# A second pair of output chunks computed with seven products, its weight sums made by accumulating transfers

## The chip, the cores and the metric

One Trainium2 chip, one core. The metric is the device time of one execution in microseconds. The program is one layer written out by hand for the five engines: TensorE (PE), VectorE (DVE), ScalarE (ACT), GpSimd (POOL) and SyncE (SP), which issues nearly all transfers.

## The reference, cut to what matters

```python
proj = jnp.einsum('bsd,de->bse', rmsnorm(x, g_norm), w_in)        # 256 x 2048 by 2048 x 7704
# ... two kinds of attention give o_moba and o_nsa, each 256 x 1024
y_moba = rmsnorm(o_moba * jax.nn.silu(m_z), g_out_moba)
y_nsa = rmsnorm(o_nsa * jax.nn.silu(n_z), g_out_nsa)
y = jnp.concatenate([y_moba, y_nsa], axis=-1)                      # 256 x 2048
return x + jnp.einsum('bse,ed->bsd', y, w_out)                     # 2048 x 2048 weights; then a last norm
```

All in float32. S = 256 tokens (two tiles m of 128), model width 2048.

## The kernel before, in words

**Units.** Both large products are cut into column chunks of 512: fifteen of w_in (chunks 0 to 14; 11 to 14 are the z chunks) and four of w_out (chunks NC to NC + 3, NC = 15, so 15 to 18 in the code, output chunks 0 to 3 in words). A unit (c, g) is chunk c by 512 rows of weights: 1 MB, and 24 matmuls of 128x512, since each of its 2 m x 4 k products is done in three terms. A weight w is split into w_hi (ACT rounds it, L1081) and w_lo = w - w_hi (DVE, L1430); x and y are split likewise; `three_products` (L692) multiplies hi by hi, hi by lo and lo by hi. So each unit goes: SP loads it into one of three buffers of w_raw once the `lo` of three units before is done (L485), ACT does `hi(u)`, DVE does `lo(u)`, PE multiplies. The split buffers w_hi and w_lo hold three places, taken in the order of RING.

**Pairs.** Where two chunks a and b form a pair, the first 512 rows of weights of both ((a, 0) and (b, 0), eight products of 6 matmuls each) are done by a Strassen-Winograd scheme with seven (`seven`, L771; P1 to P7). It needs sums of the four weight blocks B11, B12, B21, B22 (512 KB each), which DVE forms (`t1` to `t4`, L1713 to L1726), and sums of the four blocks of x or y (`x_sums`, `y_sums`). Its seven weight operands are split by `block_hi` (ACT, L1138) and `block_lo` (DVE, L1708). Partial products that both chunks need are copied out of PSUM by `mid_out_` (ACT, L1149) and added later (`mid_add`, DVE). Before the change four pairs exist: nq, Z1, Z2 and OUT_PAIR (output chunks 2 and 3).

**Slots.** Every engine runs a loop over slots (L1030, L1310, L1830) and within a slot a fixed order of calls. An engine's queue is strictly in order, so the place of a call in the loop decides what it waits behind. In general ACT and DVE round a unit in the slot given by `rounded_at` (L139), two slots ahead of PE. The stretch of the change is slots 55 to 64:

- slots 55 to 59: the last z units (14, g) on PE; the first half of y is scaled, transposed by PE in rounds (0, hg, m) (`y_round_`), multiplied with g by DVE (`y_times_g`, L1741), rounded by ACT (`y_hi`, L1281), and its remainder taken by DVE (`y_residual`, L1754). At the end of slot 59 DVE reads chunk 14 (`scaled`, L1635), ACT applies Silu (L1168), POOL multiplies with the attention's output (L651).
- slots 60 to 67: output units (0,0), (0,1), (1,0), (1,1), then (0,2), (0,3), (1,2), (1,3). Units with g of 2 or 3 need the second half of y, whose squares (L1278), root on POOL (L656 to L658), `y_scale` (L1728) and four rounds (1, hg, m) come in slots 60 to 63, two rounds at the end of slot 62 and two at the end of 63. `unit` waits for `ylo_done` and `lo_ready` (L753, L758).
- from slot 65: OUT_PAIR and its other units. The residual x is loaded into acc (= Q) at L575, and each chunk's sum is added to it (`residual`, L1763).

Of the kernel before, what the change touches and what calls it, by code (L numbers as in the profile page):

```python
# [116 lines left out]
def unit_at(slot):  # L117
# [9 lines left out]
    if slot >= NPROJ:  # L127
        c, g = OUT_UNITS[slot - NPROJ]
        return UNIT_NO[NC + c, g]
# [5 lines left out]
              41: 40, 42: 41, 43: 42, 44: 43, 45: 44, 46: 45, 47: 46, 49: 47, 50: 48, 52: 49, 53: 50, 54: 51, 55: 52, 56: 53, 57: 54, 58: 55,  # L135
              66: 61, 67: 62, 68: 63, 69: 64, 70: 65, 71: 66, 72: 67}


def rounded_at(slot):  # L139
# [4 lines left out]
    return slot - 4 if 60 <= slot < 65 else ROUNDED_AT.get(slot)  # L144
# [117 lines left out]
def heads_done(j):  # L262
# [14 lines left out]
            62: [(1, 0, 0), (1, 0, 1)], 63: [(1, 1, 0), (1, 1, 1)]}  # L277
# [10 lines left out]
def build_layer(nc, x, positions, inv_freq, w_in, g_norm, pe_ck, pe_cv, w_ck1, w_ck2, w_cv1, w_cv2,  # L288
# [4 lines left out]
    with ExitStack() as ctx:  # L293
# [3 lines left out]
        def sem(name):  # L297
# [1670 lines left out]
```

## Time and profile before

| | us |
|---|---|
| median of 3 executions | 495.52 (495.48 to 495.67) |
| the profiled execution | 495.6 |
| its span, first to last instruction | 493.8 |
| PE busy in it | 485.6, 98% of the span |
| DVE, ACT, POOL busy | 354.7, 261.9, 64.1 |
| mean granted TensorE clock | 0.998 |

The span is the part that the rows below divide; the execution's own time is 1.8 us longer. Times in the timeline count from the span's start. A busy time of PE can be longer than the distance between two starts, because matmuls overlap in the array.

### The profile page before, as it was taken

What the parts mean: (1) busy time and instruction counts of PE and PEld (TensorE: products, weight loads), DVE (VectorE), ACT (ScalarE), POOL (GpSimd) and SP (SyncE); (2) the same over time, 40 slices, a digit from 0 to 9 for tenths busy, and PEclk for the clock granted to TensorE, in tenths of its full rate; (3) what the DMA queues carried; (4) which work ended last, traced back from release to release, by engine and by line L of the source; (5) the groups of instructions that cost most, each with busy time, mean ns of one, the idle gap of its engine ahead of it and who ended that gap; (6) DMA issues with size and microseconds to landing.
All of it is one profiled execution on the core that took longest, in us unless ns stands there. A gap on an engine that the chain in (4) does not pass through costs nothing.

```text
span 493.8 us, 6550 instructions
## 1 busy us (share of the span) xinstructions
PE 485.6 (98%) x2514; PEld 403.9 (82%) x2514; DVE 354.7 (72%) x564; ACT 261.9 (53%) x374; POOL 64.1 (13%) x66
## 2 busy tenths in 40 slices
PE   9999999999999999999999999999999999999994
PEld 8887787877788888888888888888888888888883
DVE  5888855932699958775587887765887767888644
ACT  5886453642656535645544455664665664366422
POOL 2340100100112202000020200000322240040120
PEclk9999999999999999999999999999999999999999
DMA  8979894577476442433544724448247679543404
GB/s 291 335 264 383 319 330 146 197 251 260 134 270 193 171 171 85 171 129 128 171 141 158 256 61 157 140 151 304 85 144 299 240 260 360 166 150 107 147 1 170
DMA packets 56783, 97.50 MB, mean 197 GB/s; under 512 B 4560, under 2 KB 15408, under 8 KB 56368
## 3 DMA queue, kind: packets, MB, share of 16 engines
q1 hardware_dynamic: 54544, 96.03, 55.9%
q10 hardware_dynamic: 2208, 1.06, 0.9%
q8 instruction: 20, 0.33, 0.3%
q14 instruction: 11, 0.09, 0.0%
HBM read 93.93 MB, written 2.10 MB: 194 GB/s over the span
## 4 chain that ended last, share of the span: by engine, by line
PE 97%; issue 1%; DVE 0%; ACT 0%; POOL 0%; POOLq 0%; ACTq 0%; DVEq 0%
PE proj L694 26%; PE proj L696 26%; PE proj L695 26%; PE b_o L1001 4%; PE b_t L675 2%; PE b_p L970 2%; PE proj L727 2%; PE b_s L871 2%; PE proj L733 1%; PE proj L738 1%; PE proj L1021 1%; PE b_s L696 1%; PE b_s L694 1%; PE b_s L695 1%; PE b_p L675 0%
## 5 line engine op out<-in xcount | busy, mean ns | idle before, releaser
L1430 DVE TENSOR_TENSOR w_lo<-w_raw,w_hi 128x2048 fp32r<-128x2048 f32 x65 | 149.6, 2304 | 64.4 <-ACT w_hi L1081 64.3
L694 PE MATMUL proj<-w_hi,xT_hi 128*128 128x512 f32 (+1 forms) x490 | 192.6, 393 | 0.0
L696 PE MATMUL proj<-w_hi,xT_lo 128*128 128x512 f32 (+1 forms) x490 | 190.7, 389 | 0.0
L695 PE MATMUL proj<-w_lo,xT_hi 128*128 128x512 f32 (+1 forms) x490 | 190.5, 389 | 0.0
L1081 ACT ACTIVATE w_hi<-w_raw 128x2048 fp32r<-128x2048 f32 x65 | 124.1, 1912 | 32.8 <-PE proj L696 20.4
L694 PEld LDWEIGHTS proj<-w_hi,xT_hi 128*128 128x128 f32 x490 | 92.1, 188 | 20.2 <-issue 2.0
L696 PEld LDWEIGHTS proj<-w_hi,xT_lo 128*128 128x128 f32 x490 | 92.0, 188 | 19.5
L695 PEld LDWEIGHTS proj<-w_lo,xT_hi 128*128 128x128 f32 x490 | 92.1, 188 | 18.0
L1232 ACT ACTIVATE pT<-b_p 128x512 f32<-128x512 f32 (+2 forms) x24 | 11.7, 489 | 51.7 <-PE b_p L970 51.7
L642 POOL TENSOR_TENSOR rope_a<-rope_a,rope_b 128x512 f32<-128x512 f32 (+1 forms) x12 | 15.0, 1274 | 165.0 <-DVE rope_b L1517 165.0
L1711 DVE TENSOR_TENSOR w_lo<-blk_b,w_hi 128x1024 fp32r<-128x1024 f32 x16 | 19.8, 1235 | 18.3 <-ACT w_hi L1147 18.3
L694 PE MATMUL proj<-w_hi,ymT_hi 128*128 128x512 f32 x78 | 30.6, 393 | 0.0
L696 PE MATMUL proj<-w_hi,ymT_lo 128*128 128x512 f32 x78 | 30.4, 389 | 0.0
L695 PE MATMUL proj<-w_lo,ymT_hi 128*128 128x512 f32 x78 | 30.4, 389 | 0.0
L1147 ACT ACTIVATE w_hi<-blk_b 128x1024 fp32r<-128x1024 f32 x16 | 16.9, 1054 | 17.2 <-DVE blk_b L1715 11.5
L1226 ACT ACTIVATE prob<-prob,nmx 128x256 f32<-128x256 f32 (+1 forms) x48 | 21.3, 448 | 6.7 <-DVE nmx L1613 6.7
L1609 DVE CUSTOM_DVE_ANT_0 prob<-b_s,mask 128x256 f32<-128x256 f32 (+1 forms) x48 | 15.1, 352 | 8.1 <-PE b_s L696 8.1
L664 POOL TENSOR_TENSOR Q<-Q,KV 128x512 f32<-128x512 f32 x6 | 10.5, 1767 | 56.6 <-ACT rope_c L1293 56.6
L696 PEld LDWEIGHTS proj<-w_hi,ymT_lo 128*128 128x128 f32 x78 | 14.6, 188 | 3.1
L694 PEld LDWEIGHTS proj<-w_hi,ymT_hi 128*128 128x128 f32 x78 | 14.7, 188 | 2.9
L695 PEld LDWEIGHTS proj<-w_lo,ymT_hi 128*128 128x128 f32 x78 | 14.6, 188 | 2.9
L651 POOL TENSOR_TENSOR xo<-xo,rope_a 128x512 f32<-128x512 f32 x4 | 7.7, 1934 | 69.8 <-DVE xo L1633 63.7
(271 smaller groups left out, 568.4 us busy)
## 6 DMA issues: line engine op xcount, KB each, us to landing
w_raw<-in_w_in_dram SPq DMA_DIRECT2D x51, 1024.0 KB, 4.9
w_raw<-in_w_out_dram SPq DMA_DIRECT2D x14, 1024.0 KB, 5.1
xo<-in_w_ck_dram SPq DMA_DIRECT2D x4, 1024.0 KB, 8.1
xo<-in_w_cv_dram SPq DMA_DIRECT2D x4, 1024.0 KB, 7.2
w_raw<-in_w_in_dram SPq DMA_DIRECT2D x12, 256.0 KB, 5.8
Q<-in_x_dram SPq DMA_DIRECT2D x1, 2048.0 KB, 9.8
out_dram<-Q SPq DMA_DIRECT2D x8, 256.0 KB, 2.8
xo<-in_x_dram SPq DMA_DIRECT2D x3, 512.0 KB, 7.0
```

The lines of the kernel that those rows point to most:

```text
L642: nc.gpsimd.tensor_tensor(rope_a[:, m, 0:w], rope_a[:, m, 0:w], rope_b[:, m, 0:w], ALU.add).then_inc(rope_sum, 1)
L694: nc.tensor.matmul(dst, a_hi, b_hi, start=first, stop=False, skip_group_check=goes_on)
L695: nc.tensor.matmul(dst, a_hi, b_lo, start=False, stop=False, skip_group_check=goes_on)
L696: return nc.tensor.matmul(dst, a_lo, b_hi, start=False, stop=last, skip_group_check=goes_on)
L1001: last = nc.tensor.matmul(b_o[:, m * P:(m + 1) * P], a, v, start=n == 0, stop=n == len(prods) - 1)
L1081: nc.scalar.activation(split_of(u)[0], w_raw[:, u % RAW], ACT.Copy).then_inc(hi_ready, 1)
L1147: nc.scalar.activation(block_split(p, n)[0], block_raw(p, n), ACT.Copy).then_inc(blk_hi, 1)
L1226: last = nc.scalar.activation(prob[:, b, c0:c1], prob[:, b, c0:c1], ACT.Exp, bias=nmx[:, b, n:n + 1], scale=SCALE, accum_out=sums[:, b, n: ...
L1232: nc.scalar.activation(pT[:, j % 2, 0:width(j)], b_p[:, 0:width(j)], ACT.Copy).then_inc(pt_out, 1)
L1430: nc.vector.tensor_tensor(wl, w_raw[:, u % RAW], wh.bitcast(F32), ALU.subtract).then_inc(lo_ready, 1)
L1609: nc.vector.tensor_tensor_reduce(out=prob[:, j % 2, c0:c1], in0=b_s[:, c0:c1], in1=mask[:, slice(*mask_cols(j, n))], scale=1.0, scalar=NEG ...
L1711: nc.vector.tensor_tensor(lo_, block_raw(p, n), hi_.bitcast(F32), ALU.subtract).then_inc(blk_lo, 1)
```

## The change

Output chunks 0 and 1 become a fifth pair, OA. The four units (0,0), (0,1), (1,0), (1,1) of slots 60 to 63 become three slots: P1, P5 and the whole unit (1,1); then P2, P6, unit (0,1) for m = 0, P7, P3; then unit (0,1) for m = 1 and P4. All later slots are numbered one lower. The weight blocks of OA are loaded by SP into six tiles (B11 three times), and POOL adds B12, B22 and B21 onto three of them with five accumulating DMAs; the old pairs' sums on DVE change only in sign. y_sums reads the two scaled transposes in pT, in slot 56, and no longer rebuilds them from hi and lo. The mid copies of OA are added onto acc by four accumulating DMAs of POOL. The loads of x, of the OUT_PAIR blocks and of g_final move on SP. The call order of ACT and DVE between slots 56 and 62 is written anew.

Constants and the order of slots:

```diff
-OUT_UNITS = [(0, 0), (0, 1), (1, 0), (1, 1), (0, 2), (0, 3), (1, 2), (1, 3)]
+OA_SLOT = NPROJ
+OUT_UNITS = [(0, 2), (0, 3), (1, 2), (1, 3)]
-OUT_DONE = [65, 67, 71]
+OUT_DONE = [64, 66, 70]
...
-              41: 40, 42: 41, 43: 42, 44: 43, 45: 44, 46: 45, 47: 46, 49: 47, 50: 48, 52: 49, 53: 50, 54: 51, 55: 52, 56: 53, 57: 54, 58: 55,
-              66: 61, 67: 62, 68: 63, 69: 64, 70: 65, 71: 66, 72: 67}
+              41: 40, 42: 41, 43: 42, 44: 43, 45: 44, 46: 45, 47: 46, 49: 47, 50: 48, 52: 49, 53: 50, 54: 51, 55: 52, 56: 53,
+              62: 56, 63: 58, 65: 59, 66: 60, 67: 61, 68: 62, 69: 63, 70: 64, 71: 65}
...
-    return slot - 4 if 60 <= slot < 65 else ROUNDED_AT.get(slot)
+    return ROUNDED_AT.get(slot)
...
-            62: [(1, 0, 0), (1, 0, 1)], 63: [(1, 1, 0), (1, 1, 1)]}
+            61: [(1, 0, 0), (1, 0, 1)], 62: [(1, 1, 0), (1, 1, 1)]}
```

SP, the loads around unit u (unit(u) itself stands ahead of each):

```diff
+                if u == 50:
+                    sp.wait_ge(scores_done, len(JOBS))
+                    sp.dma_start(oa_t1, weight_block(OA, "B11")).then_inc(oa_in[1], 16)
+                    sp.dma_start(oa_t2, weight_block(OA, "B11")).then_inc(oa_in[2], 16)
+                    sp.dma_start(acc[:, 1, :], x[0, P:2 * P, :]).then_inc(acc_in[1], 16)
+                if u == 51:
+                    sp.dma_start(oa_b11, weight_block(OA, "B11")).then_inc(oa_in[0], 16)
+                if u == 53:
+                    sp.wait_ge(blk_sum, 4 * Z2 + 3)
+                    sp.dma_start(oa_b21, weight_block(OA, "B21")).then_inc(oa_in[4], 16)
+                if u == 54:
+                    sp.wait_ge(blk_sum, 4 * Z2 + 4)
+                    sp.dma_start(oa_t3, weight_block(OA, "B22")).then_inc(oa_in[3], 16)
+                if u == 55:
+                    sp.wait_ge(blk_lo, 7 * OA)
+                    sp.dma_start(oa_b22, weight_block(OA, "B22")).then_inc(oa_in[5], 16)
+                if u == 56:
+                    sp.wait_ge(blk_lo, 7 * OA + 2)
+                    sp.dma_start(acc[:, 0, :], x[0, 0:P, :]).then_inc(acc_in[0], 16)
...
+                if u == 58:
+                    sp.wait_ge(blk_lo, 7 * OA + 6)
+                    block(OUT_PAIR, 0)
+                    block(OUT_PAIR, 1)
```

The OUT_PAIR blocks 3 and 2 follow unit 59, and g_final follows unit 60 and a wait for block_lo(OA, 6). POOL:

```diff
+            def oa_add(n, name, tile):
+
+                pool.dma_start(tile, weight_block(OA, name), accum_op=ALU.add).then_inc(oa_sum[n], 16)
+
             for i, kind in enumerate(KINDS[:NC]):
+                if i == 12:
+                    pool.wait_ge(oa_in[1], 16)
+                    oa_add(0, "B12", oa_t1)
+                    pool.wait_ge(oa_in[2], 16)
+                    oa_add(2, "B12", oa_t2)
+                if i == 13:
+                    pool.wait_ge(oa_sum[2], 16)
+                    oa_add(3, "B22", oa_t2)
+                if i == 14:
+                    pool.wait_ge(oa_in[3], 16)
+                    oa_add(1, "B12", oa_t3)
...
+                    if i == NC - 1:
+                        pool.wait_ge(blk_lo, 7 * OA + 4)
+                        oa_add(4, "B21", oa_t2)
                     if n % 2:
                         h = n // 2
                         pool.wait_ge(y_sq, 4 * (h + 1))
...
+            for i in range(4):
+                m, c = ((0, 1), (1, 0), (0, 0), (1, 1))[i]
+                pool.wait_ge(mid_out, 4 * OA + i + 1)
+                pool.wait_ge(acc_in[m], 16)
+                pool.dma_start(acc[:, m, c * CW:(c + 1) * CW], mid_copy(OA, i), accum_op=ALU.add).then_inc(oa_added, 16)
```

PE, in slots 60, 61 and 62:

```diff
+            def oa_first():
+
+                a, b = PAIRS[OA]
+                bank_free(a)
+                pe.wait_ge(xs_lo_ok, 3)
+                seven(OA, "P1").then_inc(mid_done, 1)
+                seven(OA, "P5").then_inc(unit_used, 1)
+                bank_free(b)
+                u = UNIT_NO[b, 1]
+                pe.wait_ge(hi_ready, u - FIRST + 1)
+                pe.wait_ge(ylo_done, 3)
+                for kind, m in ((HH, 0), (LH, 0), (HL, 0), (HH, 1), (HL, 1), (LH, 1)):
+                    if (kind, m) == (HL, 0):
+                        pe.wait_ge(lo_ready, u - FIRST + 1)
+                    if (kind, m) == (HH, 1):
+                        pe.wait_ge(yhi_done, 4)
+                    if (kind, m) == (LH, 1):
+                        pe.wait_ge(ylo_done, 4)
...
+            def oa_second():
+
+                seven(OA, "P2")
+                pe.wait_ge(mid_out, 4 * OA + 1)
+                seven(OA, "P6").then_inc(mid_done, 1)
+                pe.wait_ge(mid_out, 4 * OA + 2)
+                unit_rows(UNIT_NO[PAIRS[OA][0], 1], 0).then_inc(unit_used, 1)
+                pe.wait_ge(mid_out, 4 * OA + 3)
+                seven(OA, "P7").then_inc(mid_done, 1)
+                seven(OA, "P3")
+
+            def oa_third():
+                pe.wait_ge(mid_out, 4 * OA + 4)
+                unit_rows(UNIT_NO[PAIRS[OA][0], 1], 1).then_inc(unit_used, 1)
+                seven(OA, "P4").then_inc(unit_used, 1)
```

ACT:

```diff
-                if slot == 62:
+                if slot == 57:
                     ys_round()
+                    hi(UNIT_NO[NC + 1, 1])
+                if slot == 59:
+                    block_hi(OA, 2)
+                if slot == OA_SLOT:
+                    block_hi(OA, 3)
+                    y_hi(Y_ROUNDS[57][0])
+                    mid_out_(OA, 0)
+                    mid_out_(OA, 1)
+                    hi(UNIT_NO[NC, 1])
+                    y_squares(3)
+                    block_hi(OA, 4)
+                    block_hi(OA, 5)
+                    mid_out_(OA, 2)
+                if slot == OA_SLOT + 1:
+                    mid_out_(OA, 3)
+                    block_hi(OA, 6)
...
+                if slot == 56:
+                    block_hi(OA, 0)
+                    block_hi(OA, 1)
...
                 for r in Y_ROUNDS.get(slot, []):
-                    y_hi(r)
+                    if slot != 57:
+                        y_hi(r)
+                if slot == 62:
+                    hi(UNIT_NO[NC, 3])
```

DVE:

```diff
             def y_sums():
...
+                step(nc.vector.tensor_tensor(s1, a22, a21, ALU.subtract), 9)
+                nc.vector.tensor_tensor(s3, a11, a21, ALU.add)
+                step(nc.vector.tensor_tensor(s2, s1, a11, ALU.subtract), 10)
+                nc.vector.tensor_tensor(s4, a12, s2, ALU.add).then_inc(xs_ok, 1)
...
                 for r in rounds:
                     y_times_g(r)
+                    if Y_NO[r] == 1:
+                        y_sums()
+                        dve.wait_ge(xs_ok, 3)
...
-                if slot == 64:
+                if slot == 57:
                     ys_residual()
+                    block_lo(OA, 0)
+                    block_lo(OA, 1)
+                if slot == OA_SLOT:
+                    lo(UNIT_NO[NC + 1, 1])
+                    y_parts(Y_ROUNDS[57])
+                    block_lo(OA, 2)
+                    block_lo(OA, 3)
+                    lo(UNIT_NO[NC, 1])
+                    block_lo(OA, 4)
+                    block_lo(OA, 5)
+                    y_scale(1)
+                if slot == OA_SLOT + 1:
+                    block_lo(OA, 6)
...
+                if slot == 54:
+                    y_scale(0)
+                if slot != 57:
+                    y_parts(Y_ROUNDS.get(slot, []))
+                if slot == 62:
+                    lo(UNIT_NO[NC, 3])
```

In the numbering after the change unit 54 is (1,1), 55 is (0,1), 56 is (0,2) and 57 is (0,3). The `hi` and `lo` of unit 56 stand in slot 62 by ROUNDED_AT, ahead of that slot's two rounds of y, and those of unit 57 behind them; PE multiplies unit 56 in slot 63 and unit 57 in slot 64.

## Rows read from the trace of the kernel before

**Rows 1.** The page: busy time of each engine, and the chain's shares by engine

```profile
PE 485.6 (98%) x2514; PEld 403.9 (82%) x2514; DVE 354.7 (72%) x564; ACT 261.9 (53%) x374; POOL 64.1 (13%) x66
PE 97%; issue 1%; DVE 0%; ACT 0%; POOL 0%; POOLq 0%; ACTq 0%; DVEq 0%
```

**Rows 2.** Waits of PE over the whole span: us in total, times, longest

```profile
PE proj L1021 <- POOL pT L597: 1.0, 1, 1.0
```

**Rows 3.** Timeline of PE, slots 60 to 64: start, us, engine, line, operation

```profile
398.95 0.39 PE L694 MATMUL proj<-w_hi,ymT_hi 128*128 128x512 f32 x1
...
415.05 0.39 PE L696 MATMUL proj<-w_hi,ymT_lo 128*128 128x512 f32 x1
415.28 0.60 PE L675 MATMUL b_t<-ident,xo 128*128 128x128 f32 x4
415.71 0.60 PE L675 MATMUL b_s<-ident,xo 128*128 128x128 f32 x4
416.07 0.48 PE L694 MATMUL proj<-w_hi,ymT_hi 128*128 128x512 f32 x1
...
421.63 0.60 PE L675 MATMUL b_p<-ident,xo 128*128 128x128 f32 x4
422.06 0.60 PE L675 MATMUL b_o<-ident,xo 128*128 128x128 f32 x4
422.42 0.48 PE L694 MATMUL proj<-w_hi,xT_hi 128*128 128x512 f32 x1
```

**Rows 4.** Timeline of DVE behind the first two rounds of the second half

```profile
415.91 0.69 DVE L1751 TENSOR_TENSOR pT<-b_t,ccols 128x512 f32<-128x512 f32 x1 [1.58 <-PE b_t L675]
416.52 0.68 DVE L1751 TENSOR_TENSOR pT<-b_s,ccols 128x512 f32<-128x512 f32 x1
417.30 1.29 DVE L1761 TENSOR_TENSOR xT_lo<-pT,xT_hi 128x512 fp32r<-128x512 f32 x2
419.71 2.29 DVE L1430 TENSOR_TENSOR w_lo<-w_raw,w_hi 128x2048 fp32r<-128x2048 f32 x1 [1.11 <-ACT w_hi L1081]
```

**Rows 5.** Timeline of ACT in the same stretch

```profile
416.64 1.23 ACT L1287 ACTIVATE xT_hi<-pT 128x512 fp32r<-128x512 f32 x2 [4.62 <-DVE pT L1751]
417.77 1.90 ACT L1081 ACTIVATE w_hi<-w_raw 128x2048 fp32r<-128x2048 f32 x1
```

**Rows 6.** Timeline of ACT, a mid copy and block roundings of pair Z2

```profile
352.76 1.06 ACT L1147 ACTIVATE w_hi<-blk_b 128x1024 fp32r<-128x1024 f32 x1 [0.36 <-DVE blk_b L1719]
355.25 0.68 ACT L1166 ACTIVATE rope_a<-proj,rstd 128x512 f32<-128x512 f32 x1
```

**Rows 7.** Timeline of DVE: block remainders of Z2, and chunk 14's read

```profile
355.00 1.22 DVE L1711 TENSOR_TENSOR w_lo<-raw_e,w_hi 128x1024 fp32r<-128x1024 f32 x1
356.13 1.22 DVE L1722 TENSOR_TENSOR raw_e<-raw_e,nv 128x1024 f32<-128x1024 f32 x1
...
399.15 1.41 DVE L1646 SCALAR_TENSOR_TENSOR rope_b<-proj,rstd,KV 128x512 f32<-128x512 f32 x2
```

**Rows 8.** Timeline of POOL and DVE where both read SBUF at once

```profile
347.04 4.60 POOL L651 TENSOR_TENSOR xo<-xo,rope_a 128x512 f32<-128x512 f32 x2 [63.70 <-DVE xo L1633]
347.22 3.27 DVE L1430 TENSOR_TENSOR w_lo<-w_raw,w_hi 128x2048 fp32r<-128x2048 f32 x1 [0.25 <-ACT w_hi L1081]
```

**Rows 9.** Timeline of POOL: products with z, and the root of the second half

```profile
366.87 3.66 POOL L651 TENSOR_TENSOR xo<-xo,rope_b 128x512 f32<-128x512 f32 x2 [15.23 <-ACT rope_b L1173]
...
382.46 3.07 POOL L651 TENSOR_TENSOR xo<-xo,rope_a 128x512 f32<-128x512 f32 x2 [6.11 <-ACT rope_a L1173]
...
400.65 2.57 POOL L651 TENSOR_TENSOR xo<-xo,rope_b 128x512 f32<-128x512 f32 x2 [15.11 <-ACT rope_b L1173]
404.54 0.89 POOL L656 TENSOR_TENSOR rstdy<-ssy 128x2 f32<-128x2 f32 x1 [1.32 <-ACT rope_c L1278]
...
406.64 0.87 POOL L658 TENSOR_TENSOR rstdy<-rstdy,half_c 128x2 f32<-128x2 f32 x1
```

**Rows 10.** DMA issues of the page: count, KB each, median us to landing

```profile
w_raw<-in_w_out_dram SPq DMA_DIRECT2D x14, 1024.0 KB, 5.1
raw_e<-in_w_in_dram SPq DMA_DIRECT2D x3, 512.0 KB, 8.4
```

More of the change, by code:

```diff
@@ L88, in stream @@
                 plain(c, g)
+    ring.append(("early", OA))
+    plain(NC + 1, 1)
+    ring.append(("middle", OA))
+    plain(NC, 1)
+    ring.append(("late", OA))
     for c, g in OUT_UNITS[:-1]:
@@ L412, in build_layer @@
         xs_step, xs_ok, xs_hi_ok, xs_lo_ok = sem("xs_step"), sem("xs_ok"), sem("xs_hi_ok"), sem("xs_lo_ok")
+        oa_in, oa_sum = [sem(f"oa_in{i}") for i in range(6)], [sem(f"oa_sum{i}") for i in range(5)]
+        oa_added = sem("oa_added")
         blk_hi, blk_lo, blk_sum = sem("blk_hi"), sem("blk_lo"), sem("blk_sum")
@@ L773, in seven @@
                 of, k0, m, bank_no, n, new = SEVEN[name]
+                if p == OA:
+                    n, new = OA_BLOCK[name], name in ("P1", "P5")
                 pe.wait_ge(blk_lo, 7 * p + n + 1)
-                if of == "s" and p != OUT_PAIR:
+                if of == "s" and p < OA:
                     xh, xl = [t[:, m, k0:k0 + 2, :] for t in (xs_hi, xs_lo)]
                 else:
-                    pair = (ys_hi, ys_lo) if of == "s" else (xT_hi, xT_lo) if p != OUT_PAIR else (ymT_hi, ymT_lo)
+                    pair = (ys_hi, ys_lo) if of == "s" else (xT_hi, xT_lo) if p < OA else (ymT_hi, ymT_lo)
                     xh, xl = [t[:, k0:k0 + 2, m * P:(m + 1) * P] for t in pair]
@@ L806, in pair_late @@
                 seven(p, "P4").then_inc(unit_used, 1)
+            def oa_first():
[15 more added lines that the diff above has]
+                        pe.wait_ge(ylo_done, 4)
+                    for k in range(UK):
+                        dst, y_hi_, y_lo_, wh, wl = operands(u, m, k)
+                        last = nc.tensor.matmul(dst, y_lo_ if kind == LH else y_hi_, wl if kind == HL else wh,
+                                                start=kind == HH and k == 0, stop=(kind, m) in ((HL, 0), (LH, 1)) and k == UK - 1)
+                last.then_inc(unit_used, 1)
+            def oa_second():
[11 more added lines that the diff above has]
+                seven(OA, "P4").then_inc(unit_used, 1)
             def last_chunk():
@@ L1037, in _ @@
                         pair_late(p)
+                if slot == OA_SLOT:
+                    oa_first()
+                if slot == OA_SLOT + 1:
+                    oa_second()
+                if slot == OA_SLOT + 2:
+                    oa_third()
                 if unit_at(slot) is not None:
@@ L1160, in mid_out_ @@
                     act.wait_ge(y_done, 2)
+                if p == OA:
+                    act.wait_ge(y_done, 6)
+                    nc.scalar.activation(mid_copy(p, i), mid_bank(p, i)[:, :], ACT.Copy, scale=-1.0 if i else 1.0).then_inc(mid_out, 1)
+                    return
                 if p == OUT_PAIR:
                     act.wait_ge(y_done, 8)
+                    act.wait_ge(oa_added, 64)
                     nc.scalar.activation(mid_copy(p, i), mid_bank(p, i)[:, :], ACT.Copy).then_inc(mid_out, 1)
@@ L1285, in y_hi @@
                 if half == 0:
-                    act.wait_ge(mid_done, 3 * OUT_PAIR)
+                    act.wait_ge(mid_done, 3 * OA)
                 nc.scalar.activation(dst[:, hg * HPC:(hg + 1) * HPC, m * P:(m + 1) * P],
@@ L1665, in mid_add @@
                 a = acc[:, m, c * CW:(c + 1) * CW]
-                nc.vector.tensor_tensor(a, mid_copy(OUT_PAIR, i), a, ALU.add).then_inc(mid_added, 1)
+                nc.vector.tensor_tensor(a, a, mid_copy(OUT_PAIR, i), ALU.subtract if i else ALU.add).then_inc(mid_added, 1)
             def y_sums():
-                dve.wait_ge(ylo_done, 2)
+                dve.wait_ge(yg_done, 2)
                 def step(ins, n):
@@ L1878, in _ @@
                     t2(T2_SLOT.index(slot))
-                if slot == 60:
-                    y_sums()
-                for i, at in enumerate((70, 70, 71, 71)):
+                for i, at in enumerate((69, 69, 70, 70)):
                     if slot == at:
```

100 lines of the change are left out of this document (51 added, 49 removed).

## The prediction

> **What bounds the kernel now.** I read the page first [rows 1]: PE is busy for 98% of the span and 97% of the chain that ended last is PE. The list of PE's waits [rows 2] has one entry, 1.0 us at the start; so from slot 0 on PE never waits for another engine. The timeline of PE then gives the price of a matmul: slots 60 to 62 are three units, 72 matmuls from 398.95 to 415.28, 0.227 us each [rows 3]. The time of this kernel is its count of matmuls times that pitch, as long as nothing makes PE wait. One group of two rounds of transposes takes 0.79 us (415.28 to 416.07), and slot 63 with 24 matmuls 5.56 us (416.07 to 421.63), 0.12 more than 24 pitches, since the first matmul behind transposes is slow [rows 3].
>
> **What is removed on PE.** Units (0,0) and (1,0) were 48 matmuls, P1 to P7 are 42. Six less: 6 x 0.227 = **-1.36 us**. Units, rounds of transposes and everything from the second half on are the same in number. The new order of terms in unit (1,1) keeps 24 matmuls.
>
> **The rest is a question of waits**, so I lay the new calls of ACT and DVE on the old durations. These are: `lo` 2.29, `hi` 1.90, y_times_g 0.69 with 0.61 between starts, two y_hi 1.23 [rows 4, 5]; block_hi 1.06, a mid copy 0.68 [rows 6]; block_lo 1.22 with 1.13 between starts, reading chunk 14 1.41 [rows 7]. The next operation on an engine begins about 0.1 before the one before it ends (417.87 and 417.77 on ACT), and another engine sees a result 0.04 later (419.67 on ACT, 419.71 on DVE) [rows 4, 5].
>
> *Waits in slot 63, for unit (0,2).* This is the term that decides. Call T0 the start of slot 61's transposes. Before the change rounding ran two slots ahead: behind the transposes at 415.28 the `lo` ended at 422.00, T0 + 6.72, and it was for a unit two slots on. Now the `hi` and `lo` of unit (0,2) stand behind these same rounds, and its PE work is the next slot but one, where slot 62 is only 18 matmuls. PE asks for it at T0 + 0.79 (transposes) + 18 x 0.227 + 0.12 (slot 62) + 0.79 (its transposes) = T0 + 5.78.
> What comes first on DVE is block_lo(OA, 6). It needs block_hi(OA, 6), behind mid_out_(OA, 3), which needs P7. P7 is followed only by P3 (6 matmuls, 1.36), and its last matmul ends 0.16 behind its last pitch, at T0 - 1.20. Mid copy T0 - 1.16 to - 0.48, block_hi from T0 - 0.58 to + 0.48, block_lo from T0 + 0.52 to + 1.74. So y_times_g starts at T0 + 1.66 and not at T0 + 0.63 (415.91 in rows 4), 1.03 late, and the whole old chain (y_times_g, y_hi, `hi`, `lo`) follows: `lo` ends at T0 + 6.72 + 1.03 = T0 + 7.75. PE waits 7.79 - 5.78 = **+2.0 us**. Both ends are tied to PE's own work, so nothing earlier can make up for it. Without block_lo in the way it would still be 6.76 - 5.78 = 1.0.
>
> *Waits in slot 64, for unit (0,3).* Let L be the end of that `lo`. On DVE two y_times_g follow (second one ends at L + 1.21), on ACT two y_hi, to L + 1.9, then `hi` L + 1.8 to + 3.7, then `lo` L + 3.7 to + 6.0. PE started unit (0,2) at L + 0.04 and has 5.44 of work: it waits 6.04 - 5.48 = **+0.6 us**. The unit after that, (1,2), has its `lo` at L + 8.2, PE comes at L + 11.5: no wait. From there on order and distances are those of before, one slot number lower.
>
> *Waits in slots 60 and 61.* Slot 60 begins at 398.95 as before: its blocks 0 and 1 are made in slots 56 and 57. Chunk 14 is read by 400.56 [rows 7], `lo` of unit (1,1) runs to 402.8. POOL's product with z comes at about 400.95 (block_hi(OA, 2) now stands ahead of Silu). Two such operations met before: DVE's `lo` took 3.27 and not 2.29, and two POOL operations 4.60 and not 2.57 [rows 8, 9]; one waits out the other. So POOL starts its first at 402.8 and its second at 404.0, just ahead of y_residual, which ends at 405.95 instead of 404.75. Then block_lo 2 and 3 and `lo` of unit (0,1) follow: 405.95 - 0.08 + 2 x 1.13 + 2.29 = 410.4. PE asks for block 2 at 407.1 (36 matmuls on) and gets it 0.1 late; it asks for unit (0,1) after 12 more, at 409.9, and waits 0.5. **+0.6 us**; bounds 0 (POOL's second operation waits longer) and 1.2 (a whole POOL operation).
>
> *DMAs and POOL's queue.* SP loads six weight blocks of 512 KB in place of the four in units (0,0) and (1,0), and POOL accumulates five more, 3.5 MB on top; SP's load of x is split and moved, and `unit` loads queue behind it. Four of the accumulations are early: two are issued ahead of POOL's product at 366.9, for an operand of slot 57 (387 at the earliest) and for the third, which goes ahead of the product at 382.5 for ACT at 401; the fourth goes behind that product, at 385.5, for ACT at 408.6 [rows 9]. All have over 15 us, near twice the 8.4 that a block took in a full queue [rows 10]: hidden. The fifth, B21, is issued behind block_lo(OA, 3), at 408.2, and block_hi(OA, 6) wants it at T0 - 0.6, which with the waits so far is 415.3: 7.1 us. No row has an accumulating DMA. A 1 MB load lands in 5.1, a 512 KB block in a full queue in 8.4 [rows 10]; nothing excludes a slower path that reads its target too. I take under 7.1, cost **0**, as the queue then holds one unit's load; at 8.4 it costs 1.3, at twice 5.1 it costs 3.1, and all of this falls on the wait in slot 63.
> The Trainium skill, DMA: Bandwidth & Descriptors, "Anatomy of one DMA — SWDGE (gpsimd) path", gives such a transfer 2.0 us plus its bytes at 436 GB/s; by it, an estimate, the block lands in 3.2 us and the sum stays as it is. No run here shows it yet.
> Behind that issue POOL has the root of the second half: 2.97 us (404.54 to 407.51) [rows 9] after the squares end at about 408.6, so y_scale at about 412.6, against transposes at 415.9: 2.5 us to spare for the issue itself. The four additions onto acc are issued by 417 and wanted at about 435: 0. mid_add, y_sums (one big DVE operation less) and the moved g_final load have more room than that: 0.
>
> **The sum.** -1.36 + 2.0 + 0.6 + 0.6 = +1.9 us. The profiled execution took 495.6, so 497.5; the median before is 495.52, 0.1 lower, which changes nothing: **497.5**, 0.4% slower. A difference below 0.2%, 1.0 us, I count as no change.
>
> **Rivals.**
> *B, the fifth accumulation comes late* (0.15). Its place is the wait of block_hi(OA, 6) in slot 61, and it decides from 7.1 us on. For it: two reads per byte, and SP's units and OUT_PAIR blocks beside it. Against: those start only at 410 and 412. With 8.4 to 10.2 us, 499 to 500.6.
> *C, the matmuls win* (0.10). The waits of slots 63 and 64 together stay under 0.4 us. It needs `hi` and `lo` of (0,2) ahead of y_times_g, which the order of calls excludes, or T0 earlier against PE, which it can't be. Only if I misread the order: 494.2. For it speaks that PE is the whole chain now.
> *D, half of the waits* (0.15). Slot 61 waits for nothing and block_lo(OA, 6) gets done ahead of the rounds, so only 1.0 is left in slot 63 and some tenths in slot 64: -1.36 + 1.0 + 0.5 = 495.7, no change.
>
> **How the numbers follow.** The forecast has 0.60, B 0.15, D 0.15, C 0.10. Slower by over 0.2% is forecast and B, 0.75; D is no change, 0.15; C is faster, 0.10. The range leaves out C and the upper half of B: from 495.3 (D with its second wait short) to 500.0 (the fifth accumulation at some 9.5 us).
>
> **What would show it.** PE should have 2508 matmuls, 6 fewer, and its list of waits new entries: about 2 us ahead of unit (0,2) and 0.6 ahead of (0,3), both on DVE's L1430 `lo`, and some tenths on `lo` or block_lo in slot 61. DVE's block remainder should stand directly ahead of slot 61's y_times_g, released by ACT's block_hi, and that released by PE (right) or by the DMA (B). POOL and DVE should meet at 401 to 405. I am wrong if PE is gapless there (C), if a gap stands anywhere else, such as slots 50 to 59 with its new loads, or if the granted clock leaves 2.4 GHz behind one of these waits, where before it was 0.998 of it.

## The result and the profile after

The changed kernel took 497.33 us (median of 6, 497.21 to 497.48) against 495.46 for the kernel before in the same comparison (495.37 to 495.67): +1.87 us, a ratio of 1.0037 with a 95% interval of 1.0024 to 1.005. The whole interval lies above 1.002, so by the prediction's bound of 0.2% it is slower. The forecast was 497.5. The profiled execution took 497.4, with a span of 495.6; before it was 495.6 and 493.8.

The page of the changed kernel, busy time by engine and the chain's shares; it answers to [rows 1]:

```profile
PE 484.2 (98%) x2508; PEld 401.6 (81%) x2508; DVE 357.7 (72%) x568; ACT 267.0 (54%) x383; POOL 76.0 (15%) x75
PE 91%; DVE 3%; issue 2%; ACT 2%; DMA 1%; ACTq 0%; POOLq 0%; POOL 0%; SPq 0%; DVEq 0%
```

Six matmuls fewer, 1.4 us less busy time on PE, and yet a longer span. The chain, which was PE almost alone, now runs through DVE and ACT for some per cent. The list of PE's waits (total, times, longest), which had one entry before [rows 2]:

```profile
PE proj L754 <- DVE w_lo L1567: 2.4, 3, 1.8
PE proj L1123 <- POOL pT L634: 1.0, 1, 1.0
PE proj L787 <- ACT w_hi L1194: 0.6, 1, 0.6
PE b_s L735 <- DMA xo<-in_x_dram: 0.3, 1, 0.3
```

The first line is new and is the change's: three waits for a `lo` (L1567 is L1430 before). The last two stand at the very start, where this execution was otherwise no later than the one before: slot 56's transposes begin at 387.10 here and at 387.12 there. The timeline of PE shows the three waits at their places; it answers to [rows 3]:

```profile
409.62 0.39 PE L756 MATMUL proj<-w_hi,xT_lo 128*128 128x512 f32 x1
410.33 0.47 PE L754 MATMUL proj<-w_hi,ymT_hi 128*128 128x512 f32 x1 [0.33 <-DVE w_lo L1567]
410.64 0.39 PE L755 MATMUL proj<-w_lo,ymT_hi 128*128 128x512 f32 x1
...
415.89 0.60 PE L735 MATMUL b_t<-ident,xo 128*128 128x128 f32 x4
416.33 0.60 PE L735 MATMUL b_s<-ident,xo 128*128 128x128 f32 x4
416.68 0.48 PE L754 MATMUL proj<-w_hi,ymT_hi 128*128 128x512 f32 x1
...
421.32 0.60 PE L735 MATMUL b_o<-ident,xo 128*128 128x128 f32 x4
423.67 0.47 PE L754 MATMUL proj<-w_hi,xT_hi 128*128 128x512 f32 x1 [1.76 <-DVE w_lo L1567]
...
428.98 0.39 PE L756 MATMUL proj<-w_hi,xT_lo 128*128 128x512 f32 x1
429.67 0.47 PE L754 MATMUL proj<-w_hi,xT_hi 128*128 128x512 f32 x1 [0.30 <-DVE w_lo L1567]
```

The numbers in brackets are idle time of the array; matmuls overlap, so the time lost is read from the starts. Ahead of unit (0,1) the distance is 0.71 where the pitch is 0.227: 0.48 lost. Ahead of (0,2) it is 2.35 where transposes took 0.36 in [rows 3] (422.06 to 422.42): 2.00 lost. Ahead of (0,3) it is 0.69: 0.46 lost. Two of these also make the next matmul 0.08 late (410.33 to 410.64). Together -1.36 + 0.48 + 2.00 + 0.46 + 0.16 = +1.74, and PE's last matmul starts at 488.27 against 486.47: +1.80. The account closes to 0.06 us.

The timeline of DVE in slots 60 to 62 shows what stood in the way; from 415.9 on it answers to [rows 4]:

```profile
400.46 2.28 DVE L1567 TENSOR_TENSOR w_lo<-w_raw,w_hi 128x2048 fp32r<-128x2048 f32 x1
402.66 0.69 DVE L1897 TENSOR_TENSOR pT<-b_o,ccols 128x512 f32<-128x512 f32 x1
404.04 1.67 DVE L1907 TENSOR_TENSOR ymT_lo<-pT,ymT_hi 128x512 fp32r<-128x512 f32 x1 [0.70 <-ACT ymT_hi L1402]
405.63 1.21 DVE L1850 TENSOR_TENSOR w_lo<-nv,w_hi 128x1024 fp32r<-128x1024 f32 x1
406.77 1.21 DVE L1850 TENSOR_TENSOR w_lo<-KV,w_hi 128x1024 fp32r<-128x1024 f32 x1
407.90 2.28 DVE L1567 TENSOR_TENSOR w_lo<-w_raw,w_hi 128x2048 fp32r<-128x2048 f32 x1
...
416.31 1.23 DVE L1850 TENSOR_TENSOR w_lo<-KV,w_hi 128x1024 fp32r<-128x1024 f32 x1 [1.82 <-ACT w_hi L1257]
417.45 0.68 DVE L1897 TENSOR_TENSOR pT<-b_t,ccols 128x512 f32<-128x512 f32 x1
418.05 0.68 DVE L1897 TENSOR_TENSOR pT<-b_s,ccols 128x512 f32<-128x512 f32 x1
418.83 1.29 DVE L1907 TENSOR_TENSOR xT_lo<-pT,xT_hi 128x512 fp32r<-128x512 f32 x2
421.24 2.29 DVE L1567 TENSOR_TENSOR w_lo<-w_raw,w_hi 128x2048 fp32r<-128x2048 f32 x1 [1.11 <-ACT w_hi L1189]
```

T0, the first transposes of slot 61, is 415.89 (foretold: 415.9). block_lo(OA, 6) starts at T0 + 0.42, the first y_times_g at T0 + 1.56, and the `lo` of unit (0,2) ends at 423.53, T0 + 7.64 (foretold: 0.52, 1.66 and 7.75). PE was ready at T0 + 5.78 and started 0.14 behind the end of the `lo`.

ACT in the same stretch; it answers to [rows 5]:

```profile
414.73 0.60 ACT L1273 ACTIVATE prob<-proj 128x512 f32<-128x512 f32 x1 [4.09 <-PE proj L756]
415.22 1.05 ACT L1257 ACTIVATE w_hi<-KV 128x1024 fp32r<-128x1024 f32 x1
418.17 1.23 ACT L1402 ACTIVATE xT_hi<-pT 128x512 fp32r<-128x512 f32 x2 [1.89 <-DVE pT L1897]
419.30 1.90 ACT L1189 ACTIVATE w_hi<-w_raw 128x2048 fp32r<-128x2048 f32 x1
```

ACT is idle for 4.09 us ahead of the mid copy, while the weights of unit (0,2) lie loaded (issued at 387.78, landed 8.4 us later) and its `hi` stands further back in the queue. Not all of this idle time could be used: where `hi` of (0,2) stands ahead of the mid copy (run 1 below), it waits until 413.21 for PE to free its place in w_hi:

```profile
413.21 1.92 ACT L1189 ACTIVATE w_hi<-w_raw 128x2048 fp32r<-128x2048 f32 x1 [2.81 <-PE proj L756]
```

### The profile page after: what moved, and what is told of

The parts are those of the page before. It is cut to its first block, busy times and chain, and to the rows that moved or that the text cites. A ratio compares the mean times of both kernels' runs of the same rounds, so it can differ in the third digit from the quotient of the medians.

```text
span 495.6 us, 6581 instructions
## 1 busy us (share of the span) xinstructions
PE 484.2 (98%) x2508; PEld 401.6 (81%) x2508; DVE 357.7 (72%) x568; ACT 267.0 (54%) x383; POOL 76.0 (15%) x75
## 4 chain that ended last, share of the span: by engine, by line
PE 91%; DVE 3%; issue 2%; ACT 2%; DMA 1%; ACTq 0%; POOLq 0%; POOL 0%; SPq 0%; DVEq 0%
PE proj L754 25%; PE proj L756 24%; PE proj L755 24%; PE b_o L1103 4%; PE b_t L735 2%; PE b_p L1072 2%; PE proj L787 2%; PE b_s L973 2%; PE proj L798 1%; PE proj L793 1%; DVE w_lo L1567 1%; DMA w_raw<-in_w_in_dram 1%; ACT w_hi L1189 1%; PE b_s L756 1%; PE b_s L754 1%
## 5 line engine op out<-in xcount | busy, mean ns | idle before, releaser
L754 PE MATMUL proj<-w_hi,xT_hi 128*128 128x512 f32 (+1 forms) x498 | 195.8, 393 | 2.1 <-DVE w_lo L1567 2.1
L756 PE MATMUL proj<-w_hi,xT_lo 128*128 128x512 f32 (+1 forms) x498 | 193.8, 389 | 0.0
L1567 DVE TENSOR_TENSOR w_lo<-w_raw,w_hi 128x2048 fp32r<-128x2048 f32 x63 | 145.0, 2304 | 60.4 <-ACT w_hi L1189 60.3
L1189 ACT ACTIVATE w_hi<-w_raw 128x2048 fp32r<-128x2048 f32 x63 | 120.3, 1913 | 30.2 <-PE proj L756 18.1
L754 PE MATMUL proj<-w_hi,ymT_hi 128*128 128x512 f32 x60 | 23.7, 396 | 0.3 <-DVE w_lo L1567 0.3
L756 PE MATMUL proj<-w_hi,ymT_lo 128*128 128x512 f32 x60 | 23.4, 390 | 0.0
L755 PE MATMUL proj<-w_lo,ymT_hi 128*128 128x512 f32 x60 | 23.4, 390 | 0.0
L681 POOL TENSOR_TENSOR rope_a<-rope_a,rope_b 128x512 f32<-128x512 f32 x4 | 5.6, 1394 | 60.9 <-DVE rope_b L1667 60.9
L1770 DVE COPY xo<-b_o 128x256 f32<-128x256 f32 x16 | 6.7, 420 | 10.6 <-PE b_o L1103 10.6
L1315 ACT ACTIVATE Q<-b_t 128x512 f32<-128x512 f32 x9 | 5.3, 593 | 15.8 <-PE b_t L735 15.7
```

The lines of the kernel that those rows point to most:

```text
L754: nc.tensor.matmul(dst, a_hi, b_hi, start=first, stop=False, skip_group_check=goes_on)
L755: nc.tensor.matmul(dst, a_hi, b_lo, start=False, stop=False, skip_group_check=goes_on)
L756: return nc.tensor.matmul(dst, a_lo, b_hi, start=False, stop=last, skip_group_check=goes_on)
L1189: nc.scalar.activation(split_of(u)[0], w_raw[:, u % RAW], ACT.Copy).then_inc(hi_ready, 1)
L1567: nc.vector.tensor_tensor(wl, w_raw[:, u % RAW], wh.bitcast(F32), ALU.subtract).then_inc(lo_ready, 1)
```

## The experiments

All are edits of the changed kernel; each was timed beside the kernel before, whose medians in these comparisons were 495.52 to 495.56. The question of each is whether a named wait is worth what the account says.

**1. Unit (0,2) ahead of the block and the rounds.**

```diff
-              62: 56, 63: 58, 65: 59, 66: 60, 67: 61, 68: 62, 69: 63, 70: 64, 71: 65}
+              63: 58, 65: 59, 66: 60, 67: 61, 68: 62, 69: 63, 70: 64, 71: 65}
...
                 if slot == OA_SLOT + 1:
+                    hi(56)
                     mid_out_(OA, 3)
                     block_hi(OA, 6)
...
                 if slot == OA_SLOT + 1:
+                    lo(56)
                     block_lo(OA, 6)
```

> The changed kernel, with hi of unit (0,2) ahead of the fourth mid copy on ACT and its lo ahead of block_lo(OA, 6) on DVE, in slot 61; nothing else moves. Theory (order of calls): in the changed kernel PE stands still 2.00 us ahead of unit (0,2) because that lo stands behind block_lo and the two rounds of y. Then this wait goes to 0, the one ahead of (0,3) stays at 0.4 to 0.5, and the time falls from 497.3 to 495.3. Rival (the added 3.5 MB of transfers and POOL's accumulations cost the time, the order does not matter): the weights or block 6 would be late anyway, and the time stays within 0.4 of 497.3.

Measured: 495.43 us, ratio to the kernel before 0.9998 (0.9989 to 1.0006). Two calls moved give back 1.9 us. The wait ahead of (0,2) is gone (distance 0.36); the one ahead of (0,3) became 0.53.

**2. Unit (0,3) ahead of its rounds, with and without the first move.**

```diff
+                if slot == 62:
+                    hi(UNIT_NO[NC, 3])
                 for r in Y_ROUNDS.get(slot, []):
...
-                if slot == 62:
-                    hi(UNIT_NO[NC, 3])
...
+                if slot == 62:
+                    lo(UNIT_NO[NC, 3])
                 if slot != 57:
                     y_parts(Y_ROUNDS.get(slot, []))
-                if slot == 62:
-                    lo(UNIT_NO[NC, 3])
```

Without the first move:

> The changed kernel with hi and lo of unit (0,3) ahead of slot 62's two rounds of y, and unit (0,2) left where it is. Theory (the second wait has its own cause, the rounds of y ahead of its hi): lo of (0,3) then ends at 425.8, the y remainders at 428.4, both ahead of 429.2, the 0.46 us wait ahead of (0,3) goes, the 2.00 ahead of (0,2) stays, and the time is 496.8. Rival (the second wait is only an echo of the first): no change, 497.3.

Measured: 496.81 us, ratio 1.0026 (1.0016 to 1.0036), as foretold. The second wait has a cause of its own.

With the first move:

> As the run with unit (0,2) moved, and hi and lo of unit (0,3) ahead of slot 62's rounds too. Theory: both waits go; the list of PE's waits keeps only the 0.5 us in slot 61, and the time is 497.3 - 2.0 - 0.46 - 0.15 (first matmul behind each wait) = 494.7, below the kernel before (495.5). The y rounds come later by one lo each, but are wanted at 421.7 and 427.2 and end at about 420.4 and 426.4. Rival: they are late instead (a new wait on the y remainder in place of the one removed), and the time is 495.3 or more.

Measured: 495.12 us, ratio 0.9992 (0.9983 to 1.0), 0.4 above the forecast and nearer to the rival. DVE and PE of that run:

```profile
422.44 2.29 DVE L1568 TENSOR_TENSOR w_lo<-w_raw,w_hi 128x2048 fp32r<-128x2048 f32 x1 [1.11 <-ACT w_hi L1189]
...
426.03 1.29 DVE L1908 TENSOR_TENSOR xT_lo<-pT,xT_hi 128x512 fp32r<-128x512 f32 x2
```

```profile
427.38 0.50 PE L754 MATMUL proj<-w_hi,xT_hi 128*128 128x512 f32 x1
427.72 0.40 PE L755 MATMUL proj<-w_lo,xT_hi 128*128 128x512 f32 x1
```

The y remainders end at 427.32, not 426.4, and PE starts unit (0,3) 0.48 after the matmul before it: 0.25 us of a new wait in place of the old. The remainders of the rounds before were already 0.9 late (421.32, not 420.4), so the delay comes from slot 61: `hi` of (0,2) waited for PE to free its place until 413.35, its `lo` began at 415.30, and from there DVE worked without a gap to 421.32. Ahead of the `lo` of (0,3) DVE was then idle for 1.11 us, because ACT's `hi` stands behind y_hi of the rounds before; run 9 makes use of that.

**3. The block between y_times_g and y_residual.**

```diff
-                if slot == OA_SLOT + 1:
-                    block_lo(OA, 6)
...
                 for r in rounds:
                     y_times_g(r)
...
+                if rounds and Y_NO[rounds[0]] == 4:
+                    block_lo(OA, 6)
                 for r in rounds:
                     y_residual(r)
```

> The changed kernel with block_lo(OA, 6) between the two y_times_g and the two y_residual of slot 61 instead of ahead of all four. Theory: y_times_g starts right behind the transposes, 1.03 us sooner, and with it y_hi, hi and lo of unit (0,2); the wait ahead of that unit falls from 2.00 to about 1.0, and the time to 496.3. P4 wants the block at T0 + 3.6 and gets it at T0 + 3.1. Rival (block_lo is not on the path, hi of unit (0,2) waits for its place in w_hi or for its load): no change, 497.3.

Measured: 496.46 us, ratio 1.0019 (1.001 to 1.0028). The distance ahead of unit (0,2) is 1.44 and not 2.35, so the block's place was worth 0.9 of the 2.0, by the order of two DVE calls alone. Neither the place in w_hi nor the load of (0,2) held it up.

**4. The first wait: the early lo.**

```diff
                     block_lo(OA, 0)
                     block_lo(OA, 1)
+                    lo(UNIT_NO[NC + 1, 1])
                 if slot == OA_SLOT:
-                    lo(UNIT_NO[NC + 1, 1])
                     y_parts(Y_ROUNDS[57])
```

> The changed kernel with one DVE call moved: lo of unit (1,1) from slot 60 to the end of slot 57, where DVE has 1.3 us free ahead of chunk 14's read. Theory: DVE's chain in slot 60 is a chain from 399.1 on with no gap; this takes 1.2 us out of it, the wait ahead of unit (0,1) (0.48 us) goes, the waits of slots 63 and 64 stay, and the time is 496.8. Rival (the wait in slot 61 comes from ACT, whose hi of unit (0,1) ends at 406.8): no change, 497.3.

Measured: 496.76 us, ratio 1.0025 (1.0016 to 1.0034): 0.57 for the 0.48 and its slow first matmul. The waits of slots 63 and 64 stayed at 2.00 and 0.46. The move did two things at once. The `lo` of (0,1) began 1.07 sooner (406.83), although DVE now stood idle for 1.57 us ahead of y_residual, waiting for ACT. And POOL's two products, no longer beside a `lo`, took 2.56 us in all and not 4.03, so that y_residual took 1.04 and not 1.67.

**5. The first wait: POOL's second product beside y_residual.**

```diff
+                        w = 8 if i == NC - 1 and m else CW
-                        nc.gpsimd.tensor_tensor(xo[:, m, n * CW:(n + 1) * CW], xo[:, m, n * CW:(n + 1) * CW],
-                                                z[:, m, :], ALU.mult).then_inc(y_done, 1)
+                        nc.gpsimd.tensor_tensor(xo[:, m, n * CW:n * CW + w], xo[:, m, n * CW:n * CW + w],
+                                                z[:, m, 0:w], ALU.mult).then_inc(y_done, 1)
```

> The changed kernel in which POOL's product of chunk 14 for m = 1 covers 8 of its 512 columns; the rest of that product is left out, so the output is another. Theory (POOL's second operation holds the read port that DVE's y_residual needs in slot 60, which took 1.67 us and not 0.69): y_residual takes 0.7, DVE's chain up to lo of unit (0,1) ends 1.0 sooner, the 0.48 us wait in slot 61 goes, and the time is 496.8. Rival (y_residual was long for another reason, such as the accumulating DMAs): no change, 497.3.

Measured: 496.7 us, ratio 1.0024 (1.0015 to 1.0033). DVE of this run, slot 60:

```profile
403.94 0.69 DVE L1908 TENSOR_TENSOR ymT_lo<-pT,ymT_hi 128x512 fp32r<-128x512 f32 x1 [0.70 <-ACT ymT_hi L1403]
404.55 1.22 DVE L1851 TENSOR_TENSOR w_lo<-nv,w_hi 128x1024 fp32r<-128x1024 f32 x1
405.68 1.22 DVE L1851 TENSOR_TENSOR w_lo<-KV,w_hi 128x1024 fp32r<-128x1024 f32 x1
406.82 2.29 DVE L1568 TENSOR_TENSOR w_lo<-w_raw,w_hi 128x2048 fp32r<-128x2048 f32 x1
```

y_residual took 0.69 and not 1.67, all behind it came 1.0 sooner, and PE did not wait in slot 61. The long y_residual was POOL's doing. Runs 4 and 5 remove the same 0.48 us, so their gains don't add up.

**6. Silu ahead of the block.**

```diff
-                if slot == 59:
-                    block_hi(OA, 2)
...
                 if slot == OA_SLOT:
+                    block_hi(OA, 2)
                     block_hi(OA, 3)
```

> The changed kernel with ACT's Silu of chunk 14 ahead of block_hi(OA, 2), so that POOL's two products could start at 400.6 instead of 401.1. Theory (the one that comes first holds the port to its end): DVE's lo of unit (1,1), from 400.46, still comes first, POOL's first product waits for it until 402.7, its second meets y_residual as before, and the time stays 497.3. Rival (block_hi ahead of Silu is what shifts POOL onto y_residual): POOL is done sooner, and 496.8 comes out.

Measured: 497.47 us, ratio 1.0039 (1.0026 to 1.0051), so no change. POOL's two products:

```profile
400.48 4.52 POOL L703 TENSOR_TENSOR xo<-xo,rope_b 128x512 f32<-128x512 f32 x2 [12.21 <-ACT rope_b L1288]
```

In the changed kernel the same row reads:

```profile
401.13 4.03 POOL L703 TENSOR_TENSOR xo<-xo,rope_b 128x512 f32<-128x512 f32 x2 [12.40 <-ACT rope_b L1288]
```

POOL starts 0.65 sooner (0.16 of it because this whole stretch runs that much earlier here) and takes 0.49 longer: DVE's `lo` began 0.18 ahead of it, and POOL ends 4.70 us behind the start of that `lo` in both kernels. y_residual takes 1.67 us again.

**7. The accumulations as plain loads.**

```diff
-                pool.dma_start(tile, weight_block(OA, name), accum_op=ALU.add).then_inc(oa_sum[n], 16)
+                pool.dma_start(tile, weight_block(OA, name)).then_inc(oa_sum[n], 16)
```

> The changed kernel with POOL's five accumulating DMAs of weights as plain loads of the same blocks into the same tiles at the same places; the weight sums are thereby left out, so the output is another. It measures what the accumulating form costs. Theory: all five are hidden, the fifth by 0.8 us (it lands 6.1 us after its issue, at 414.4, and ACT wants it at 415.2), so the time stays 497.3, and the landing times of the five show the price of the form. Rival (the accumulating form loads the DMA engines or POOL's queue and so delays the chain in slots 60 to 62): 496.9 or less.

Measured: 497.41 us, ratio 1.0036 (1.0023 to 1.0049), no change, and PE's three waits stand at 0.45, 2.00 and 0.47. Time to landing of the fifth, in the changed kernel:

```profile
KV<-in_w_out_dram POOLq DMA_DIRECT2D x1, 512.0 KB, 6.1
```

and as a plain load:

```profile
KV<-in_w_out_dram POOLq DMA_DIRECT2D x1, 512.0 KB, 3.9
```

The others, in order of issue, landed in 7.2, 10.7, 10.0 and 9.1 us accumulating and in 5.7, 6.5, 7.4 and 5.0 as plain loads. The differences are 1.5 to 4.2 us per block, and none of it reaches PE here. They are not the price of the form alone: the fourth, for one, was issued at 387.52 in the changed kernel and at 385.66 here, because the plain load that fills its tile first landed later in the changed kernel.

The accumulations also slow what goes out beside them. The 1 MB load of a z unit, issued by SP at 360.1, landed in 11.3 us in the changed kernel and in 7.8 with plain loads, and ACT's `hi` waited for it (0.74 us), which it did in neither the kernel before nor this run:

```profile
371.42 1.92 ACT L1189 ACTIVATE w_hi<-w_raw 128x2048 fp32r<-128x2048 f32 x1 [0.74 <-DMA w_raw<-in_w_in_dram]
```

PE had enough ahead of it there and did not wait. The transfers are hidden, but they are not free.

**8. The fifth accumulation twice.**

```diff
                         nc.gpsimd.tensor_tensor(rstdy[:, h, :], rstdy[:, h, :], half_c[:, :], ALU.pow).then_inc(rstdy_ok, 1)
+                    if i == NC - 1:
+                        pool.wait_ge(oa_sum[4], 16)
+                        oa_add(4, "B21", oa_t2)
...
-                    act.wait_ge((oa_in[0], oa_sum[0], oa_in[4], oa_sum[3], oa_sum[1], oa_in[5], oa_sum[4])[n], 16)
+                    act.wait_ge((oa_in[0], oa_sum[0], oa_in[4], oa_sum[3], oa_sum[1], oa_in[5], oa_sum[4])[n], 32 if n == 6 else 16)
```

> The changed kernel with the fifth accumulation (B21) done a second time, issued once the first has landed and behind the root of the second half of y on POOL; ACT's block_hi(OA, 6) waits for both. The sum then holds B21 twice. Theory: the second lands about 6 us after 414.4, at 420.5, ACT has wanted it since 415.2, and block_lo, P4, the rounds of y and unit (0,2) all follow it: 5.3 us, 502.6. With it the room of the fifth accumulation is shown to be below 1 us. Rival (there is more room, since PE waits for the lo of (0,2) in any case): 500 or less.

Measured: 506.2 us, ratio 1.021 (1.0194 to 1.0227), 3.6 above the forecast. ACT and PE of this run:

```profile
423.22 1.06 ACT L1260 ACTIVATE w_hi<-KV 128x1024 fp32r<-128x1024 f32 x1 [7.96 <-DMA KV<-in_w_out_dram]
```

```profile
425.59 0.79 PE L757 MATMUL proj<-w_hi,ymT_hi 128*128 128x512 f32 x1 [5.98 <-DVE w_lo L1853]
426.18 0.63 PE L758 MATMUL proj<-w_lo,ymT_hi 128*128 128x512 f32 x1
426.60 0.63 PE L759 MATMUL proj<-w_hi,ymT_lo 128*128 128x512 f32 x1
```

The second transfer was issued at 414.44 and its block was rounded from 423.22, 8.8 us on; the size I had set was 6. The likely reason is company: the four additions onto acc went out behind it from 415.27 on, and the DMA engines were busy throughout (the DMA share in the rows at the end of this document is 1.03 and 1.13). No run separates this from other causes. block_hi comes 8.0 later than in the changed kernel, and so do y_times_g and the `lo` of (0,2) (429.23 against 421.24): the chain follows the transfer one for one. The rest, 0.9 us between the medians, is TensorE's clock, below. The step of this expectation that failed is the transfer's duration; the place where it is waited for was right.

**9. All three moves, and a version that beats both kernels.**

> The changed kernel with the two moves of the run with (0,2) and (0,3) ahead and the early lo of unit (1,1) together. Theory (the waits are separate and add up): 495.1 less the 0.55 that the early lo was worth alone gives 494.6; PE's only wait left between slots 60 and 64 is some 0.25 us on the y remainder ahead of (0,3). Rival (the waits share slack, so that removing one lengthens another): 495.1.

Measured: 494.56 us, ratio 0.9981 (0.9972 to 0.999). The waits add up. The last one, on the y remainders, is filled in by one more move, on top of these three:

```diff
                 if slot == 62:
+                    y_times_g((1, 1, 0))
                     lo(UNIT_NO[NC, 3])
+                    y_times_g((1, 1, 1))
+                    for r in Y_ROUNDS[slot]:
+                        y_residual(r)
-                if slot != 57:
+                elif slot != 57:
                     y_parts(Y_ROUNDS.get(slot, []))
```

> The kernel with all three moves, and in slot 62 DVE does y_times_g of the first round ahead of lo of unit (0,3) instead of behind it, where it had 1.1 us of idle time. Theory: the y remainders end 0.6 us sooner, the last 0.25 us wait goes, and PE is gapless from slot 1 on: the time is the count of matmuls alone, 495.5 - 1.36 = 494.1 to 494.3. Rival (something else than the waits in slots 61 to 64 costs time, for instance the 3.5 MB more of transfers): 494.6 or more.

Measured: 494.2 us (494.14 to 494.39), ratio 0.9973 (0.9963 to 0.9983). The whole list of PE's waits in this run:

```profile
PE proj L1123 <- POOL pT L634: 1.0, 1, 1.0
PE proj L787 <- ACT w_hi L1194: 0.6, 1, 0.6
```

Nothing is left between slots 60 and 64. The time is 1.34 us below the kernel before (495.54), against six matmuls at 0.227, which are 1.36. All eleven DMAs of OA's weights and the four additions are still in it, and none of their time reaches the end.

## Why the prediction was right, point by point

- *What bounds the kernel* held: a wait of PE anywhere between slots 60 and 64 moved the end by its own length (and the 0.08 us of a slow first matmul where it has one), in each run but run 8, where the clock added to it.
- *-1.36 us for six matmuls* is what remains when no wait is left: -1.34 (run 9).
- *+2.0 us in slot 63*, the deciding term, measured 2.00. Run 1 took it away, and run 3 split it as the working did: 1.03 for block_lo(OA, 6) foretold, 0.9 found, the rest for the rounds of y that the `lo` stood behind. The agreement to a hundredth is partly luck. The `lo` ended 0.11 sooner than foretold, because the mid copy took 0.60 and not 0.68; and PE started 0.14 behind its end, where the working had 0.04, read between ACT and DVE. (At the two other waits PE started 0.15 behind the `lo`.)
- *+0.6 us in slot 64* measured 0.46, with its own cause (run 2, first part). The working gave PE 5.44 us of work in slot 63, where its own row had 5.56 with the slow first matmul; 5.54 was measured.
- *+0.6 us in slots 60 and 61* measured 0.48. The mechanism, POOL's second product ahead of y_residual, is shown by run 5, and that POOL's earlier start changes nothing by run 6. The `lo` of (0,1) ended at 410.18, not 410.4, and PE started 0.15 behind it. The expected 0.1 for block 2 did not come: the block ended at 406.84, and PE was there at 407.10.
- A term was missing: the first matmul behind a wait is followed 0.08 us late, 0.16 in all. The terms as measured add up to +1.74, the forecast's to +1.84; the two waits that were set 0.26 too long in all and the 0.16 left out nearly cancel, so the total agrees better than its parts.
- *The fifth accumulation* had 6.9 us between issue (408.28) and want (415.22), foretold 7.1, and landed in 6.1. Cost 0 was right, with 0.8 us to spare, but no row had shown an accumulating DMA, and the size was a choice. The four others took 7.2 to 10.7 us in fuller queues; at 10.7 the fifth would have cost 3.8 us. That it stayed under 7 is in part luck, and rival B was that close; run 8 shows what lies behind it.
- The estimate by the Trainium skill, DMA: Bandwidth & Descriptors, "Anatomy of one DMA — SWDGE (gpsimd) path", 3.2 us for that block, is short for both forms: 3.9 plain and 6.1 accumulating (run 7). The measurement decides.
- Rival C needed under 0.4 us in slots 63 and 64 together, and 2.46 were found. Rival D needed no wait in slot 61, where PE waited 0.48, and block_lo(OA, 6) done before the rounds, where it ended 1.65 behind T0 (417.54) and held up the first y_times_g.

## What to carry to other kernels

Where an engine's queue is in order, removing work from the bounding engine shortens the cover of everything that stood behind it; lay the calls of the other engines on the new, shorter slots and ask at each wait what stands ahead of the call that ends it. Here the transfers, which look like the expensive part of the change, stayed hidden, the closest with 0.8 us to spare, and the places of a few calls cost 3.1 us. A wait tied on both ends to the same engine (its own transposes at one end, its next unit at the other) can be worked out closely before anything is run; here each step of it was within 0.1 to 0.15 us.

## What the runs showed of the hardware that was not expected

An accumulating DMA from POOL takes markedly longer than the plain one: 6.1 against 3.9 us for 512 KB in a quiet stretch (DMA share 0.11 from 408 to 411 in the changed kernel), 7.2 to 10.7 against 5.0 to 7.4 in busier ones (the changed kernel and run 7). While the second was in flight, the DMA engines were fully busy in both kernels but moved fewer bytes with the accumulating form, by the last number (GB/s) of the changed kernel's row and of run 7's:

```profile
363.00:366.00 3.00, 3.00 (x14) 2.46 (x14) 3.00 (x3) 1.38 (x2) 0.00 (x0) 1.00 1.08 206
363.00:366.00 3.00, 3.00 (x14) 2.46 (x14) 3.00 (x3) 1.38 (x2) 0.00 (x0) 1.00 0.99 357
```

The clock. PE stood for 6.1 us in run 8 (the starts are 419.22 and 425.59, less one pitch). The stretches of 5 us from 415 on, all engines (the number ahead of the last two is the granted clock, then the DMA share and GB/s):

```profile
415.00:420.00 5.00, 4.61 (x25) 3.56 (x23) 0.00 (x0) 0.26 (x1) 4.27 (x5) 1.00 1.03 342
420.00:425.00 5.00, 0.00 (x0) 0.00 (x0) 0.69 (x1) 1.06 (x1) 0.00 (x0) 0.73 1.13 205
425.00:430.00 5.00, 4.16 (x14) 3.24 (x14) 3.79 (x6) 3.03 (x3) 0.00 (x0) 0.59 0.46 83
430.00:435.00 5.00, 3.33 (x10) 2.65 (x11) 4.01 (x5) 2.84 (x3) 0.00 (x0) 0.75 0.39 146
435.00:440.00 5.00, 5.00 (x22) 4.08 (x21) 4.49 (x2) 2.92 (x3) 0.00 (x0) 0.91 0.96 327
```

The granted clock falls from 1.00, which is 2.4 GHz, behind the long stand, and the matmuls then start 0.43 us apart (426.18 to 426.60) and not 0.227: the lower level, 1.2 GHz. The low level comes in two stretches: the clock is 0.50 from 423 to 429, back at 1.00 for 430 to 432, and 0.50 again from 433 to 435. Two rows of single microseconds:

```profile
430.00:431.00 1.00, 0.00 (x0) 0.00 (x0) 1.00 (x1) 0.00 (x0) 0.00 (x0) 1.00 0.00 0
434.00:435.00 1.00, 1.00 (x4) 0.76 (x3) 0.12 (x1) 1.00 (x1) 0.00 (x0) 0.50 1.05 410
```

The first, to 429, costs nothing at the end: PE then waits for the `lo` of (0,2) anyway and starts that unit at 431.67, 8.00 later than in the changed kernel (423.67). The second lies inside slot 63, which takes 7.14 us (431.67 to 438.81) and not 5.54. That is 1.60 more, of which 0.53 stand in place of the wait ahead of (0,3) and its slow first matmul. PE's last matmul starts at 497.33 against 488.27, 9.06 later in this execution: the 8.0 of the transfer and 1.1 of the clock (0.9 between the medians). The waits of 2.00 us in the changed kernel left the clock at 1.00. So a long wait of PE can cost more than its own length.
